# One encoder block with 32 experts: the gather of tokens written straight as transposed columns, router columns kept outside the weight ring, and the first expert's item count read earlier

## What is computed

```python
logits = (xt @ w_router + b_router)             # 256 tokens, 32 experts
top_val, top_idx = lax.top_k(logits, 4)
gates = jax.nn.softmax(top_val, axis=-1)
# for each expert e, for the tokens that chose it:
gu = xb @ w_gate_up[e] + b_gate_up[e]           # 1024 x 2048 weights
gate, up = jnp.split(gu, 2, axis=-1)
gate = jnp.minimum(gate, 7.0); up = jnp.clip(up, -7.0, 7.0)
hmid = (up + 1.0) * (gate * jax.nn.sigmoid(1.702 * gate))
out = hmid @ w_down[e] + b_down[e]              # 1024 x 1024 weights
y[token] += gate_of_token * out
```

## Time and profile before

| what | value |
|---|---|
| median of the runs | 1203.18 us |
| profiled execution, time | 1202.36 us |
| profiled execution, span of the trace | 1200.6 us |
| TensorE busy | 1165.7 us, 97% of the span |
| weights read from memory | 438.45 MB, 366 GB/s over the span |
| mean granted TensorE clock | 0.995 of full speed |

### The profile page before, as it was taken

How to read it: one execution, slowest core, us unless ns; L and a number is a source line. 1 busy time by engine, 2 the same in 40 slices (tenths; PEclk the granted TensorE clock), 3 DMA queues, 4 the chain that set the end, 5 groups by cost and what they waited for, 6 DMA issues and landing times.

```text
span 1200.6 us, 14108 instructions
## 1 busy us (share of the span) xinstructions
PE 1165.7 (97%) x5359; PEld 492.7 (41%) x5359; DVE 302.0 (25%) x680; ACT 214.7 (18%) x404; POOL 6.6 (1%) x13
## 2 busy tenths in 40 slices
PE   9999999999999999999999999999999999999996
PEld 4476556854333333333333333333333333333332
DVE  3456543246221111111211111111111121111112
ACT  2120551221111111111111111111111111112112
POOL 0000010000000000000000000000000000000000
PEclk9999999999999999999999999999999999999999
DMA  9800279338999999999999999999999999999994
GB/s 359 363 1 1 105 273 343 155 141 316 424 427 427 427 433 430 426 438 427 431 430 432 430 427 432 435 427 432 413 427 435 432 430 429 426 426 429 428 423 180
DMA packets 32019, 440.28 MB, mean 367 GB/s; under 512 B 4832, under 2 KB 5088, under 8 KB 13952
## 3 DMA queue, kind: packets, MB, share of 16 engines
q1 hardware_dynamic: 31104, 439.32, 86.9%
q10 hardware_dynamic: 864, 0.19, 0.1%
HBM read 438.45 MB, written 1.05 MB: 366 GB/s over the span
## 4 chain that ended last, share of the span: by engine, by line
PE 85%; DMA 11%; ACT 2%; DVE 1%; issue 1%; POOLq 0%; ACTq 0%
PE quad L1559 33%; PE quad L1583 17%; DMA ring<-in_w_gate_up 11%; PE y_banks L1524 5%; PE quad L1508 4%; PE y_banks L1343 2%; PE y_banks L1157 2%; PE quad L1157 2%; PE quad L1516 2%; ACT work L641 2%; PE y_banks L1179 1%; PE y_banks L1249 1%; PE y_banks L1320 1%; PE quad L1328 1%; PE quad L1454 1%; PE y_banks L1454 1%
## 5 line engine op out<-in xcount | busy, mean ns | idle before, releaser
L1559 PE MATMUL quad<-ring,work 128*64 128x512 f32 x2112 | 464.8, 598 | 7.0 <-DMA ring<-in_w_gate_up 6.7
L1559 PEld LDWEIGHTS quad<-ring,work 128*64 128x64 f32 x2112 | 150.6, 138 | 298.6 <-issue 286.4
L1583 PE MATMUL quad<-ring,work 128*64 128x512 f32 x1056 | 233.9, 595 | 10.9 <-ACT work L641 10.9
L1583 PEld LDWEIGHTS quad<-ring,work 128*64 128x64 f32 x1056 | 87.3, 137 | 144.3 <-issue 118.4
L1098 DVE TENSOR_SCALAR work<-quad 128x512 f32<-128x512 f32 x33 | 22.8, 691 | 307.7 <-PE quad L1559 307.7
L637 ACT ACTIVATE work<-work 128x512 f32<-128x512 f32 x33 | 20.8, 630 | 438.7 <-DVE work L1098 438.7
L1013 DVE CAST work<-cst 96x64 bf16 (+1 forms) x34 | 6.5, 191 | 278.6 <-PE quad L1559 278.6
L1524 PE MATMUL y_banks<-work 64*128 64x512 f32 x272 | 67.6, 615 | 0.7 <-ACT work L647 0.7
L1508 PE MATMUL quad<-h,work 128*64 128x512 f32 x272 | 64.3, 593 | 0.0
L645 ACT ACTIVATE work<-quad 128x512 f32<-128x512 f32 x33 | 19.7, 597 | 243.3 <-PE quad L1583 243.3
L637 ACT ACT_TABLE_LOAD x33 | 42.3, 1283 | 1.1 <-issue 0.5
(11 more groups left out here) (269 smaller groups left out, 824.1 us busy)
## 6 DMA issues: line engine op xcount, KB each, us to landing
ring<-in_w_gate_up SPq DMA_DIRECT2D x37, 4096.0 KB, 32.5
ring<-in_w_gate_up SPq DMA_DIRECT2D x52, 2048.0 KB, 23.0
ring<-in_w_down SPq DMA_DIRECT2D x18, 4096.0 KB, 31.4
ring<-in_w_down SPq DMA_DIRECT2D x25, 2048.0 KB, 21.9
ring<-in_w_mkv SPq DMA_DIRECT2D x8, 1024.0 KB, 23.6
ring<-in_w_in SPq DMA_DIRECT2D x7, 976.0 KB, 17.0
ring<-in_w_down SPq DMA_DIRECT2D x12, 512.0 KB, 10.7
ring<-in_w_o SPq DMA_DIRECT2D x1, 4096.0 KB, 13.0
```

Source lines behind the costliest of these rows:

```text
L1559: ins = mm(bank[n // 2][lo:lo + BLK, :], xgT[:, k % 4 * P + k // 4 * BLK:k % 4 * P + k // 4 * BLK + BLK], up_rows(j, k)[:, n * 512:(n + 1) ...
L1583: ins = mm(bank[3][n * BLK:(n + 1) * BLK, :], lhs, down_rows(j, f)[:, n * 512:(n + 1) * 512], start=(f == 0), stop=(f == KC - 1))
```

## The change

The router's columns move out of the ring (into `pair_area` and `turn_area`), so chunk 10 is issued along with chunk 7, after `om_mm`. The first expert's item index comes from the counts (`last0_i`, one more VectorE copy), after `counts_ready`; `ends_ready` is waited for at the second expert. `gather` swaps its operands: `h` in slices of 128 columns is stationary, `pick` (64 columns) moves, and 16 matmuls write bank 2 as columns that `gathered_out` reads at once. `gathered_copy`, `gathered_columns` and their semaphores go, and the hidden values' transposes use bank 3.

```diff
-        h3T_s = spl(kT_flat, KC)
...
+        h3T = [a.rearrange("p (k q) -> p k q", q=P) for a in (pair_area(0, D), turn_area(D, D))]
+        square_late = pair_area(D, 512), turn_area(512, 512)
...
             load_chunk(7)
+            load_chunk(10)
             sp.wait_ge(S["wm_mm"], 4)
             load_chunk(8)
             sp.wait_ge(S["wm_mm"], 5)
             load_chunk(9)
-            sp.wait_ge(S["rt_mm"], 2)
-            load_chunk(10)
...
-            sp.wait_ge(S["ends_ready"], 1)
-            lasts = {0: last_of(0)}
+            sp.wait_ge(S["counts_ready"], 1)
+            lasts = {0: sp.value_load(last0_i[0:1, :], min_val=0, max_val=NITEM - 1)}
             for e in range(1, NE):
+                if e == LEAD:
+                    sp.wait_ge(S["ends_ready"], 1)
...
-            def gathered_copy(w):
-
-                act.wait_ge(S["gathered"], w + 1)
-                act.activation(xg_s, bank[2][:, :], ACT.Copy).then_inc(S["xg_copied"], 1)
...
-                dve.wait_ge(S["xgT_mm"], w + 1)
+                dve.wait_ge(S["gathered"], w + 1)
...
-                                      bank[3][:, :].rearrange("p (c n s) -> p c n s", c=4, n=2)[:, i:i + m, :, :],
+                                      bank[2][:, :].rearrange("p (c n s) -> p c n s", c=4, n=2)[:, i:i + m, :, :],
...
+            dve.tensor_copy(last0_i, extra[:, 0:1])
...
-            def gather(w):
-
-                for t in range(TT):
-                    pe.wait_ge(S["pick_ready"], w * TT + (t + 1))
-                    for n in range(2):
-                        ins = mm(bank[2][n * BLK:(n + 1) * BLK, :], pick[:, t, :], h[:, t, n * 512:(n + 1) * 512],
+            def gather(first=False):
+
+                for k in range(KC):
+                    lo = k % 4 * P + k // 4 * BLK
+                    for t in range(TT):
+                        if first and k == 0:
+                            pe.wait_ge(S["pick_ready"], t + 1)
+                        ins = mm(bank[2][:, lo:lo + BLK], h[:, t, k * P:(k + 1) * P], pick[:, t, :],
                                  start=(t == 0), stop=(t == TT - 1))
                 ins.then_inc(S["gathered"], 1)
-
-            def gathered_columns(w):
-
-                pe.wait_ge(S["xg_copied"], w + 1)
-                for c in range(4):
-                    ins = pe.transpose(bank[3][:, c * P:(c + 1) * P], xg_s[:, c * P:(c + 1) * P], ident)
-                ins.then_inc(S["xgT_mm"], 1)
...
                 pe.wait_ge(S["gsel_ready"], w + 1)
-                gather(w + 1)
+                pe.wait_ge(S["pick_ready"], w * TT + 2 * TT)
+                gather()
                 pe.wait_ge(S["out_copied"], w + 1)
                 scatter().then_inc(S["scattered"], 1)
-                gathered_columns(w + 1)
                 pe.wait_ge(S["hmid_ready"], w + 1)
                 for c in range(4):
-                    ins = pe.transpose(bank[2][:, c * P:(c + 1) * P], h_s[:, c * P:(c + 1) * P], ident)
+                    ins = pe.transpose(bank[3][:, c * P:(c + 1) * P], h_s[:, c * P:(c + 1) * P], ident)
                 ins.then_inc(S["hid_mm"], 1)
                 biases(w + 1)
                 pe.wait_ge(S["hid_ready"], w + 1)
-                pe.wait_ge(S["xg_ready"], w + 3)
...
                 pe.wait_ge(S["gtok_ready"], w + 1)
+                pe.wait_ge(S["xg_ready"], w + 3)
```

More of the change, by code:

```diff
@@ L209, in encoder_kernel @@
         kT96 = spl(pair_area(2048, HEADS * SEQ), HEADS)
-        gate_s, up_s, sig_s, xg_s = (pair_area(512 * i, 512) for i in range(4))
+        gate_s, up_s, sig_s = (pair_area(512 * i, 512) for i in range(3))
         h_s = up_s
@@ L235, in encoder_kernel @@
         probT_m = prob_area(1024, 2 * TT * SEQ).rearrange("p (j m q) -> p j m q", j=2, m=TT)
-        square_late = pair_area(0, 512), pair_area(512, 512)
+        h3T = [a.rearrange("p (k q) -> p k q", q=P) for a in (pair_area(0, D), turn_area(D, D))]
+        square_late = pair_area(D, 512), turn_area(512, 512)
         wr = spl(pair_area(1536, KC * NE), KC)
@@ L257, in encoder_kernel @@
             om_mm om_ready wm_mm h2_ready h2_sq h3T_mm h3T_ready rt_mm
-            xg_copied xgT_mm mask_ready rank_mm gate_in gate_e gates_ready gtT_mm gtT_ready counts_ready
+            mask_ready rank_mm gate_in gate_e gates_ready gtT_mm gtT_ready counts_ready
             chunks_used parts_used gathered xg_ready scattered hid_mm hid_ready out_copied gsel_mm gsel_ready
@@ L288, in encoder_kernel @@
         first_i = rt[:, 1128:1129].bitcast(i32)
+        last0_i = rt[:, 1129:1130].bitcast(i32)
         total_f, items_i = rt[:, 1088:1089], rt[:, 1089:1090].bitcast(i32)
@@ L628, in _ @@
                 act.activation(ex[:, t, :], lg[:, t, :], ACT.Exp, bias=nmax0[:, t:t + 1]).then_inc(S["gate_e"], 1)
-            gathered_copy(0)
             act.wait_ge(S["gtT_mm"], 1)
-            act.activation(gT[0:NE, :], bank[2][0:NE, 0:SEQ], ACT.Copy).then_inc(S["gtT_ready"], 1)
+            act.activation(gT[0:NE, :], bank[3][0:NE, 0:SEQ], ACT.Copy).then_inc(S["gtT_ready"], 1)
             act.wait_ge(S["counts_ready"], 1)
@@ L637, in _ @@
                 act.activation(sig_s, gate_s, ACT.Sigmoid, scale=ALPHA).then_inc(S["sig_ready"], 1)
-                gathered_copy(w + 1)
                 act.wait_ge(S["hid_mm"], w + 1)
-                act.activation(hT, bank[2][:, :], ACT.Copy).then_inc(S["hid_ready"], 1)
+                act.activation(hT, bank[3][:, :], ACT.Copy).then_inc(S["hid_ready"], 1)
                 act.wait_ge(S["chunks_used"], w * NCH + NCH)
@@ L976, in columns @@
                 dve.wait_ge(S["h3T_mm"], 2 * t + b + 1)
-                with_gain(h3T_s[:, 4 * b:4 * b + 4, t * P:(t + 1) * P], spl(bank[2 + 2 * t + b][:, :], 4),
+                with_gain(h3T[t][:, 4 * b:4 * b + 4, :], spl(bank[2 + 2 * t + b][:, :], 4),
                           G_MOE + 4 * b, 4, P).then_inc(S["h3T_ready"], 1)
@@ L1466, in router @@
                 for k in range(4 * b, 4 * b + 4):
-                    ins = mm(bank[t][:, 0:NE], h3T_s[:, k, t * P:(t + 1) * P], wr[:, k, :], start=(k == 0), stop=(k == KC - 1))
+                    ins = mm(bank[t][:, 0:NE], h3T[t][:, k, :], wr[:, k, :], start=(k == 0), stop=(k == KC - 1))
                 return ins
@@ L1598, in _ @@
             residual_in(1, 1)
-            gather(0)
+            gather(first=True)
             pe.wait_ge(S["counts_ready"], 1)
             first = pe.value_load(first_i[0:1, :], min_val=1, max_val=NITEM - 1)
-            gathered_columns(0)
             pe.wait_ge(S["gates_ready"], 2)
             for t in range(TT):
-                ins = pe.transpose(bank[2][0:NE, t * P:(t + 1) * P], gates_e[:, t, :], ident)
+                ins = pe.transpose(bank[3][0:NE, t * P:(t + 1) * P], gates_e[:, t, :], ident)
             ins.then_inc(S["gtT_mm"], 1)
```

## The result

The changed kernel takes **1239.84 us** (median of 5 runs), the kernel before 1203.18: a ratio of 1.029 with an interval of 1.028 to 1.031, some 37 us slower. The forecast was 1234, with 1224 to 1262 as its range. In one execution every matmul took over twice as long from the first to the last, and that was the one profiled; the profile shown here is of the same kernel run again (run e1_after, 1238.83 us, profiled span 1237.0).

The account below looks back on a forecast made before the run. TensorE was taken as the bound, the weight stream close behind. 1202.36 + 41.2 for 33 items - 10 of stalls + 0.2 before the first item gave 1233.8, forecast as 1234 us, range 1224 to 1262.

Parts of the forecast that it names:

- The mechanism: In the swapped gather, 128-column stationary loads set record spacing, TensorE stays the bound: 1224 to 1240 us, chance 0.73.
- Hidden loads: Rival: gather loads hide at 55 to 58 ns a record, the weight stream bounds: about 1197 us, chance 0.10.
- added-up loads: Rival: load and moving columns add up to 133 ns a gather record: 1261.6 us, chance 0.07.
- the 81 ns: Rival: gather records spaced 81 ns, the Trainium skill's figure, some 3 us of stalls remaining: 1209 us, chance 0.05.
- gather, an item: Gather in each item: 32 records at 107 ns take 3.42 us for 1.72, 1.70 us more.
- ScalarE's copy to down product: Ahead of the down product: removing the wait for xg_ready, thought hidden behind ScalarE's copy, gains nothing.
- stalls for weights: TensorE's waits for weights in the expert stage: longer items let the stream keep up, so 10 us come back.
- up to the first item: Before the first item: longer gather, copy and transposes gone, later VectorE parts: 0.2 us more, between 0 and 0.6.
- the three neighbours of 101, 106 and 109 ns: Trace rows with 1, 32 and 128 moving columns, used to set the gather's spacing at 107 ns.
- One sign: Expected in the profile after: the DMA share falls under 1.00 in the later items.
- The load edits: Earlier chunk 10 and first refill: weights 5 to 6.5 us earlier, worth 0 with TensorE as bound, all with the stream.
- The clock: Drop behind the down biases stays; rival: the half-empty array in the gather lowers it every item, 1290 us, chance 0.05.

Follow-up runs that it names:

- e1_after: The changed kernel itself, with the whole change against the kernel before, run again for its profile: 1238.83 us, profiled span 1237.0.
- e4_half_moving: The changed kernel with only 32 of the 64 places moving in each gather matmul, leaving out half of each item's token selection: 1263.66 us.
- e10_halves_half_moving: The changed kernel with gather loads of 64 columns on alternating column halves of the array and only 32 places moving: 1200.19 us, ratio 0.997 to the kernel before.
- e3_gather: The kernel before with only the swapped gather, its loads of weights left as before: 1239.71 us.
- e8_gather_twice: The changed kernel with the gather's 16 matmuls done twice in each item: 1355.80 us.

## Why the prediction was right, and where it was off

**The mechanism.** Right. The stationary loads set the spacing (e4_half_moving, e10_halves_half_moving), TensorE is the bound with the swapped gather, and the gather alone makes the loss (e3_gather). Hidden loads (55 to 58 ns), added-up loads (133) and the 81 ns are all refuted by the 112 ns of the second gather in e8_gather_twice. The Trainium skill's other figure, in TensorE: Matmul & The Clock Gate, section LDWEIGHTS (loading the stationary operand), gives a load in ns as its columns divided by 1.2, an estimated 107 ns for 128 and 53 for 64. The runs agree within 10%: 112, and 58.

**The sizes, term by term.** Over the stage the profiled span grew by 1237.0 - 1200.6 = 36.4 us; the sum had 31.4.

| term | forecast | measured |
|---|---|---|
| gather, an item | +1.70 (107 ns) | +1.99 (112 ns and 0.15 fixed) |
| transposes, an item | -0.45 | -0.44 |
| ScalarE's copy to down product | 0 | -0.19 |
| item | +1.25 | +1.38 |
| 33 items | +41.2 | +45.5 |
| stalls for weights | -10 | -10 |
| up to the first item | +0.2 | +0.7 |

The term that was off is the size of a gather record. I set it between the three neighbours of 101, 106 and 109 ns; the run of 32 takes 112, and the change of shape 0.15 us more, for which I had no term. Together they are 0.29 us an item, 9.6 in all. The 112 could have been read before the run. The 101 and 106 are not spacings: I divided runs of 8 and 16 records by their number, and in both the second record starts only 0.03 us behind the first. The other records of the same two runs start 111 to 113 ns apart, with 1 column moving and with 32. Two rows show it, one from the trace before, its 8 records 279.98 - 279.07 = 0.91 us or 114 ns each, and one from the chain of e1_after (112 ns):

```profile
279.07 1.08 PE L1467 MATMUL quad<-work,ring 128*128 128x32 f32 x8
279.98 1.96 PE L1473 MATMUL y_banks<-h,cst 128*128 128x512 f32 x4
```

```profile
279.93 0.67 PE quad L1463 x6
```

So the rise from 101 to 106 ns, which the prediction takes for an effect of the columns, is one of the length of the run. Only the third neighbour, the transposes, is really a little quicker: 109 ns. Part of the 9.6 us was covered by an error the other way: I took the wait for `xg_ready` ahead of the down product as hidden behind ScalarE's copy, and counted its removal as nothing. Before, 25.8 us of the down product's weight loads' idle time ended with VectorE's L1021, and the product started 0.23 us behind the copy; after, 0.04. That is 0.19 us an item, 6 us in all. It was measured only together with the rest of the swap; what exactly holds the load for 0.19 us when two waits follow each other was not tried alone. That the two errors have opposite signs is luck: with the first alone the time would have come out 6 us later, near 1246, outside the 1224 to 1240 that I gave this case and inside the stated range. As it is, 1239.84 lies at the very end of the 1224 to 1240.

**Before the first item.** The first gate/up starts at 287.98, not 287.24. About 0.45 us were there before the gather began (283.49 in the chain, 283.04 before) and stand in the chain at 246 us already (246.39 for 245.94), ahead of anything the change touches: executions differ by as much, and the first gather record starts between 282.6 and 283.7 us in the traces here. The other 0.3 is the change's. In the first item the second gather waits for VectorE's `pick` until 302.03: the new gather wants both token tiles at once. It comes after the tables of item numbers, which VectorE builds from 289.6 to 297.2, and cost about 0.1 us beyond an ordinary item's share (28.48 against 27.02, 1.46 for 1.38). The prediction did not name it.

**The stalls.** Right: 10 us came back, by lead counted in items. No wait for weights is left in the profile after. They were not all waits: behind one of them, 2.5 us of idle time, the granted clock dropped a second time (0.72 over 5 us, so partly at 1.2 GHz), which the prediction overlooked and which went with the stalls. The row is of the kernel before:

```profile
788.00:793.00 5.00, 2.49 (x8) 0.77 (x8) 0.00 (x0) 0.00 (x0) 0.00 (x0) 0.72 1.02 439
```

One sign did not come: the DMA share is under 1.00 only where the ring is full, from 840 to 880 us, and not in the later items.

**The load edits.** Worth 0 under the swapped gather, as forecast. The sentence beside it, that with the stream as the bound they are worth all of 5 to 6.5 us, is wrong: alone they gave 2 to 3. It overlooked that the lead is capped by the 11 slots. A chunk that lands earlier in a ring that is going to be full before the first slot is freed starts nothing earlier.

**The clock.** With 64 columns moving it never dropped in an ordinary item, with 32 in every second one. The drop behind the down biases stayed in the profiled execution (0.77 from 744 to 750 us), as forecast.

## What to carry to other kernels

Before swapping a matmul's operands, count the columns that are loaded, not only those that move: a run of whole-array float32 loads with few moving columns goes at the load's pace, 112 ns a record here, whether 1, 32 or 64 columns move. If the output can be cut into two column halves of the array, the loads of the two overlap, and the same work costs half; here it took back the whole loss of 36 us. Read a spacing from the starts of records inside a run, not from the run's length over its number. And where two resources are within a few per cent of each other, as TensorE and the weight stream here, most of a loss on the one counts (36 of 45 us), while a gain ends at the other: 24 us less TensorE work bought 1.2.

## What the hardware showed beyond that

- The granted clock fell behind a run of 32 records whose loads took 3.69 us and that moved 32 columns each, in 16 of 33 items (0.57 over the next 3.3 us, 1.6 us lost each time), and did not fall with 64 columns, not even behind 64 such records in 7.3 us. Cutting work from a load-bound stretch made the kernel 25 us slower. With 64-column loads on two halves and 32 columns moving (1.84 us of it) the ordinary items kept their 26.37 us.
- A matmul that is the first of a whole-array run behind column-half pairs costs about 0.15 us more than its successors (3.72 and 3.57 us for the same 32 records).
